# Seven block products in the second input projection: five rwkv blocks and three gate pairs, ten gate tiles left to the weave

## The chip, the cores and the metric

One NeuronCore of one Trainium2 chip runs the kernel. The metric is the device time of one execution in microseconds. TensorE (PE) multiplies, VectorE (DVE), ScalarE (ACT) and GpSimd (POOL) do the rest, and SyncE (SP) issues all DMAs from one queue.

## The reference

Two transformer-like blocks run one behind the other on 1024 tokens of 1024 channels, in float32. The change lies in the second block's input projection, cut here to what matters:

```
h = rmsnorm_2(x, g_mix)
z = h @ w_in                       # 1024 x (672 + 1792 + 2048) columns
z_mla, z_rwkv, z_gate = split(z)
z_rwkv = z_rwkv + (shifted by one token - z_rwkv) * mu_rwkv
gate = sigmoid(z_gate)
y_a = mla_branch(z_mla, ...)       # attention over two scaled latents, q and kv
y_b = rwkv7_branch(z_rwkv, ...)    # r, k, v of 512 columns each, ranks of 256
x = x + (gate_a * y_a + gate_b * y_b) @ w_out
```

## The kernel before

Every large product is made of three float32r matmuls: hi x hi, hi x lo and lo x hi, where ScalarE rounds an operand to its hi part (`split_hi`) and VectorE subtracts to get the lo part (`split_lo`). Activations stand transposed (channels on partitions, tokens along the row) as `op`, hi and lo of eight 128-channel tiles. A matmul multiplies a 128x128 weight tile with 512 tokens (one half) into one of eight PSUM banks, which `tile_of` hands out in turn.

The projection stage has one generator for each engine (`z_sync`, `z_tensor`, `z_scalar`, `z_vector`, `z_gpsimd`), and the engines meet by semaphores only; each works through its own list in order. Its blocks of 256 output columns come in the order: three of the latents (`lat`), then seven of rwkv (`rwkv_blocks` = 6, 2, 3, 0, 1, 4, 5). `dense` (L892 to L894) makes a block of 4 output tiles of 128x512 from 8 channel tiles, 96 matmuls. Between the matmuls of rwkv blocks one and two `norm_q` and `norm_kv` put the column sums and the spread of the latents' norms on PE. VectorE drains each bank to `z_row` with the token scale `rs`, and shifts a tile by two operations (`z_shift`, a subtraction at L183 and a scalar_tensor_tensor at L193). SyncE stores it to DRAM. The latents are scaled in place in `lat` by `scale_latent` and stored for later.

The 2048 gate columns are not made there. `wkv_tensor` blends 32 half tiles of gates (24 matmuls each, L2591 to L2593; `gate_steps`, tiles in `wt_g`) with `weave(front, back)`: four of them ahead (`GATE_LEAD`), the others spread evenly over 16 steps of the first front alone and 20 steps of each of four backs. A front prepares a pair of rwkv heads (ranks, norms, decays, mostly on VectorE and ScalarE, with single matmuls between); the back of pair p makes its scores while the front of pair p+1 runs. So each front has a chain PE, ScalarE, VectorE, PE, and the gate products stand between its links in PE's list. VectorE drains each gate half with `rs`, ScalarE takes the sigmoid (L2608).

A seven-product form exists already (class `Sevens`, `sevenfold`, `seven_products`, used by both feed-forwards, L915 to L918). It splits channels, columns and tokens in two each and makes 7 products of 4 channel tiles, 128 columns and 512 tokens, 84 matmuls, where 8 blocks take 96. It needs four sums of weight quarters (`add_all`), seven hi and lo parts of weights, seven forms of the moving operand (`x`), and sums of the products: of each pair ScalarE keeps three banks (`kept`) and VectorE adds the others. In the feed-forward three weight buffers stand in turn.

## Time and profile before

| what | us |
|---|---|
| three runs, lowest, median, highest | 2754.94, 2759.53, 2760.14 |
| the profiled execution | 2758.2 |
| its span from the first to the last instruction | 2756.4 |
| PE busy | 2645.3 (96%) |
| VectorE, ScalarE, GpSimd busy | 1792.2, 987.7, 400.3 |

A stretch is read by the table of busy time (Rows 2): PE's busy time against the length tells whether PE has gaps. A matmul's record is longer than its turn, since matmuls overlap: the distance of two starts is what one costs. A row of the timeline gives start, duration, engine, line, operation, tiles, shape and count, and in brackets the idle time before it with what ended it.

### The profile page before, as it was taken

The page shows a single profiled execution, that of the slowest core. Times are in us where ns is not written, and L with a number is a line of the kernel's source. Part 1 is how long each engine was busy: PE and PEld are TensorE (multiplying, and loading weights), DVE is VectorE, ACT ScalarE, POOL GpSimd, SP SyncE. Part 2 cuts the span into 40 slices and gives each one's busy share as a digit, 9 for nine tenths or more (in the row PEclk, how much of TensorE's full clock was granted, in tenths as well). Part 3 has the DMA queues.
Part 4 walks back from the last instruction along what each step waited for, and adds up shares of the span by engine and source line. Part 5 has one row for each costly group of instructions (what it writes and reads, how often), then busy time and mean ns, then how long its engine had stood idle before and what let it go on. Part 6 is the DMA issues. An engine that isn't in the chain of part 4 may idle for free.

```text
span 2756.4 us, 37636 instructions
## 1 busy us (share of the span) xinstructions
PE 2645.3 (96%) x15032; PEld 2140.6 (78%) x15032; DVE 1792.2 (65%) x2291; ACT 987.7 (36%) x1352; POOL 400.3 (15%) x345
## 2 busy tenths in 40 slices
PE   7989999999999999999999899889999999999998
PEld 6777888888787878877778577678888887888876
DVE  7795677777666565445553856645498886766554
ACT  5244443333333421024444543332343233433422
POOL 2001122222200000000002602303112221000211
PEclk9999999999999999999999999989999999999999
DMA  5332223233487513245557234243234447986411
GB/s 192 48 115 99 77 85 110 97 111 104 149 317 278 186 62 136 88 138 151 170 156 208 61 81 167 93 161 135 87 125 148 162 149 252 347 325 218 143 40 62
DMA packets 302445, 401.93 MB, mean 146 GB/s; under 512 B 66017, under 2 KB 180577, under 8 KB 299969
## 3 DMA queue, kind: packets, MB, share of 16 engines
q1 hardware_dynamic: 302272, 399.53, 42.8%
q8 instruction: 120, 1.97, 0.3%
q14 instruction: 53, 0.43, 0.0%
HBM read 278.51 MB, written 121.21 MB: 145 GB/s over the span
## 4 chain that ended last, share of the span: by engine, by line
PE 83%; DVE 9%; ACT 3%; issue 3%; DMA 1%; POOL 1%; SPq 0%; DVEq 0%; ACTq 0%; POOLq 0%
PE bank L915 8%; PE bank L918 8%; PE bank L916 8%; PE bank L1986 6%; PE bank L892 6%; PE bank L1987 6%; PE bank L1988 6%; PE bank L893 6%; PE bank L894 6%; PE bank L2591 2%; PE bank L3326 2%; PE bank L2592 2%; PE bank L2593 2%; PE bank L3356 1%; PE bank L4051 1%
## 5 line engine op out<-in xcount | busy, mean ns | idle before, releaser
L915 PE MATMUL bank<-hi,hi 128*128 128x512 f32 x1008 | 393.0, 390 | 2.7 <-ACT kept L2042 1.4
L183 DVE TENSOR_TENSOR w_lo<-w_raw,w_hi 128x2048 fp32r<-128x2048 f32 (+4 forms) x123 | 256.0, 2097 | 142.7 <-ACT w_hi L480 98.2
L1986 PE MATMUL bank<-w_hi,w_hi 128*128 128x512 f32 x756 | 296.3, 392 | 9.1 <-DVE w_lo L183 6.6
L1987 PE MATMUL bank<-w_lo,w_hi 128*128 128x512 f32 x756 | 295.7, 391 | 0.0
L1988 PE MATMUL bank<-w_hi,w_lo 128*128 128x512 f32 x756 | 295.6, 391 | 0.0
L892 PE MATMUL bank<-op_hi,w_hi 128*128 128x512 f32 x608 | 238.9, 393 | 2.4 <-DVE gates L950 1.5
L893 PE MATMUL bank<-op_lo,w_hi 128*128 128x512 f32 x608 | 237.4, 390 | 0.0
L894 PE MATMUL bank<-op_hi,w_lo 128*128 128x512 f32 x608 | 237.4, 390 | 0.0
L918 PE MATMUL bank<-hi,block_lo 128*128 128x512 f32 x576 | 224.1, 389 | 0.0
L916 PE MATMUL bank<-block_lo,hi 128*128 128x512 f32 x576 | 224.1, 389 | 0.0
L915 PEld LDWEIGHTS bank<-hi,hi 128*128 128x128 f32 x1008 | 189.4, 188 | 43.6 <-ACT kept L2042 2.2
L183 POOL TENSOR_TENSOR sq_sum<-sq_sum,sq 128x1024 f32<-128x1024 f32 (+1 forms) x33 | 70.0, 2121 | 1013.6 <-ACT sq L735 1012.2
L183 POOL TENSOR_TENSOR f_out<-f_out,rs 128x512 f32<-128x512 f32 x78 | 129.0, 1653 | 416.8 <-DVE f_out L183 362.4
L183 DVE TENSOR_TENSOR block_lo<-block,hi 128x512 fp32r<-128x512 f32 (+1 forms) x168 | 133.3, 803 | 82.7 <-ACT hi L580 75.4
L2042 ACT ACTIVATE kept<-bank 128x512 f32<-128x512 f32 x108 | 64.6, 598 | 330.1 <-PE bank L918 330.0
L1986 PEld LDWEIGHTS bank<-w_hi,w_hi 128*128 128x128 f32 x756 | 142.8, 189 | 40.6 <-DVE w_lo L183 7.8
L916 PE MATMUL bank<-sum_lo,hi 128*128 128x512 f32 x432 | 168.1, 389 | 0.0
L918 PE MATMUL bank<-hi,sum_lo 128*128 128x512 f32 x432 | 168.1, 389 | 0.0
L1988 PEld LDWEIGHTS bank<-w_hi,w_lo 128*128 128x128 f32 x756 | 142.9, 189 | 29.8
L1987 PEld LDWEIGHTS bank<-w_lo,w_hi 128*128 128x128 f32 x756 | 143.0, 189 | 29.6
L183 DVE TENSOR_TENSOR hT<-hT,bank 128x512 f32<-128x512 f32 x88 | 58.2, 684 | 120.1 <-PE bank L1988 62.7
L892 PEld LDWEIGHTS bank<-op_hi,w_hi 128*128 128x128 f32 x608 | 114.7, 189 | 27.3 <-issue 3.4
(518 smaller groups left out, 5563.3 us busy)
## 6 DMA issues: line engine op xcount, KB each, us to landing
f_scratch<-f_out SPq DMA_DIRECT2D x189, 256.0 KB, 2.0
w_raw<-f_scratch SPq DMA_DIRECT2D x42, 1024.0 KB, 9.7
w_raw<-in_w_ffn_down SPq DMA_DIRECT2D x28, 1024.0 KB, 5.7
record<-record_scratch SPq DMA_DIRECT2D x16, 1024.0 KB, 5.4
block<-in_w_ffn_up SPq DMA_DIRECT2D x16, 1024.0 KB, 5.5
w_raw<-in_w_down SPq DMA_DIRECT2D x14, 1024.0 KB, 5.3
w_raw<-in_w_in SPq DMA_DIRECT2D x13, 1024.0 KB, 6.2
block<-in_w_gate SPq DMA_DIRECT2D x11, 1024.0 KB, 5.2
```

Source lines behind the costliest of these rows:

```text
L183: return e.tensor_tensor(out, x, y, op)
L892: t.matmul(ps[:], hi[:, k, wc], x[0][:, k, xc], start=n == 0, stop=False)
L893: t.matmul(ps[:], hi[:, k, wc], x[1][:, (k + turn) % KD, xc], start=False, stop=False)
L894: last = t.matmul(ps[:], lo[:, k, wc], x[0][:, k, xc], start=False, stop=n == kt - 1)
L915: t.matmul(ps[:], w.hi(q, n)[:, j, :], x.hi(i, n)[:, j, :], start=start, stop=False, skip_group_check=more)
L916: t.matmul(ps[:], w.hi(q, n)[:, j, :], x.part(i, n, lo=1)[:, j, :], start=False, stop=False, skip_group_check=more)
L918: last = t.matmul(ps[:], w.part(q, n, lo=1)[:, j, :], x.hi(i, n)[:, j, :], start=False, stop=end, skip_group_check=more)
L1986: t.matmul(ps[:], ws[0][:, j, wc], xs[0][:, j, :], start=start, stop=False, skip_group_check=more)
L1987: t.matmul(ps[:], ws[0][:, j, wc], xs[1][:, j, :], start=False, stop=False, skip_group_check=more)
L1988: last = t.matmul(ps[:], ws[1][:, j, wc], xs[0][:, j, :], start=False, stop=stop, skip_group_check=more)
L2042: s.activation(F.kept[n // 2][:], psum.tile(F.name, "x", q)[:], ACT.Copy).then_inc(*A.up("kept", q, n))
L2591: t.matmul(ps[:], hi[:, k, :], op[0][:, k, hs(half)], start=k == 0, stop=False)
```

## The change

Of the seven rwkv blocks two (6 and 2) stay plain. Behind them eight pairs of column tiles are made in seven products: three gate pairs (tiles 0 to 5) and then the rwkv blocks 3, 0, 1, 4, 5. The weights come by `Sevens` with two buffers of 1 MB (`w_z`), a pair's load waiting for the last product of two pairs before. The moving operand has seven forms (`xz`): three are blocks of `op`, four (2, 3, 4, 5) are made during the plain blocks, each 128 x 4 x 512: GpSimd makes three sums of blocks and the three operations of form 5, VectorE three subtractions and four lo parts, ScalarE four hi parts. Each is waited for by the first pair's product that uses it.

For each pair ScalarE keeps three banks, VectorE makes four halves of `z_row` (one with `rs`, three sums), GpSimd multiplies the three sums by `rs`. VectorE shifts an rwkv pair (`pair_shift`) behind the pair's last product, ScalarE takes a gate pair's sigmoid there (`gated`). The weights of the first two woven gate tiles are split behind the last shift. The column sums of both latents now lie in plain block one and only the spread for kv in block two. The store of the latents has three semaphores in place of one, and the loads of ranks, masks and the first r and k are split in two groups (`load_ranks`, `load_first`) behind products of the last two pairs. The weave gets ten gate tiles, 20 halves, spread over the same steps.

```diff
@@ class Memory
+        self.w_z = self.sevens(P, 4, tuple(66 + n for n in range(7)), [(s, (s + 4, s + 5, s + 6)) for s in (82, 9)])
+        self.x_z = {n: (at(lo, "x_raw", [P, 4, HALF]), at(hi, "x_hi", [P, 4, HALF], F32R), at(lo, "x_lo", [P, 4, HALF], F32R))
+                    for n, lo, hi in ((2, 90, 94), (3, 98, 78), (4, 18, 22), (5, 26, 30))}
@@ build
-    plan += [wblock(w_in2, 0, KD, MLA_COLS + 256 * i, 256) for i in rwkv_blocks]
+    plan += [wblock(w_in2, 0, KD, MLA_COLS + 256 * i, 256) for i in rwkv_blocks[:PLAIN_BLOCKS]]
...
-                   [wblock(w_in2, 0, KD, MLA_COLS + RWKV_COLS + P * i, P) for i in range(16)], before)
+                   [wblock(w_in2, 0, KD, MLA_COLS + RWKV_COLS + P * i, P) for i in range(2 * GATE_PAIRS, 16)], before)
...
+    z_pairs = [("gate", g) for g in range(GATE_PAIRS)] + [("rwkv", b) for b in rwkv_blocks[PLAIN_BLOCKS:]]
+    z_order, z_last = list(sevenfold(len(z_pairs))), len(z_pairs) - 1
...
+    def turned_over(k):
+        q, n = z_order[k]
+        return [(q1, n1) for q1, n1 in ([(q, 0)] if n == 2 else []) + ([z_order[k - 1]] if k and z_order[k - 1][1] else [])
+                if q1 < z_last]
@@ z_sync
+            if 0 <= pair < z_last - 1:
+                q.wait_ge(*Sz.T.of("zup", pair, 6))
+                wz.load(q, pair + 2, pair_source(pair + 2))
...
+            store_rows(m)
@@ z_tensor
+        for q, n in z_order:
+            if n == 2:
+                t.wait_ge(*A.of("z kept", q, 0))
+            if n == 4:
+                t.wait_ge(*A.of("z kept", q, 2))
+            if n == 5:
+                t.wait_ge(*A.of("z kept", q, 4))
+            if n == 6:
+                t.wait_ge(*V.of("z sum", q, 4))
+            if q == 0 and n in mem.x_z:
+                t.wait_ge(*V.of("form lo", n))
+            seven_products(t, T, "zup", "zs", q, n, wz, xz, 0)
@@ z_scalar
+        form_hi(2)
+        landed(s, *d_lat)
+        form_hi(4)
+        s.wait_ge(*wt1.used(B_RWKV + 1))
+        form_hi(3)
...
+            for q1, n1 in turned_over(k):
+                s.wait_ge(*T.of("zup", q1, n1))
+                wz.split_hi(s, q1 + 1, n1)
+            if k and z_order[k - 1][1] == 6:
+                gated(z_order[k - 1][0])
@@ z_vector
+        rows_out(0)
         v.wait_ge(*V.last())
+        shift(0, 0)
+        shift(0, 1)
+        scale_latent("kv", 3, 2, vec["g_kv_a_2"])
+        yield
+        landed(v, *d_xk)
+        wz.landed(v, 1)
+        wz.add_all(v, 1)
+        for n in (0, 1):
+            wz.split_lo(v, 0, n)
+        landed(v, d_lat[1])
+        for n, x, y, row, col in ((4, x_raw[2], x_raw[3], 1, 1), (3, x_raw[3], mem.x_even[:], 0, 0), (2, x_raw[2], x_raw[3], 1, 1)):
...
+            tt(v, x_raw[n], x, y, ALU.subtract).then_inc(*V.up("form", n))
+        form_lo(2)
+        for n in (2, 3, 4):
+            wz.split_lo(v, 0, n)
+        form_lo(4)
+        rows_out(1)
+        form_lo(3)
+        shift(1, 0)
+        shift(1, 1)
+        yield
+        for k, (q, n) in enumerate(z_order):
+            if n == 2 and 1 < q + 1 <= z_last:
+                wz.landed(v, q + 1)
+                wz.add_all(v, q + 1)
+            for q1, n1 in turned_over(k):
+                wz.split_lo(v, q1 + 1, n1)
+            if k and z_order[k - 1][1] == 6:
+                pair_shift(z_order[k - 1][0])
+            if n in Z_HALVES:
+                z_sum(q, n)
+            if k == 3:
+                form_lo(5)
+                for j in (5, 6):
+                    wz.split_lo(v, 0, j)
+            yield
+        pair_shift(z_last)
+        wt_g.split_lo(v, 0)
+        wt_g.split_lo(v, 1)
@@ z_gpsimd
+        block(x_raw[2], 1, 1)
...
+        block(x_raw[3], 0, 1)
+        g.wait_ge(*Sz.T.of("cols q"))
+        block(mem.x_even[:], 0, 0)
+        landed(g, *d_lat)
+        g.wait_ge(*Sz.A.of("form hi", 2))
+        tt(g, x_raw[5], op_block(0, 1, 0), xz.hi(0, 2), ALU.subtract).then_inc(*G.up())
...
+        tt(g, x_raw[5], x_raw[5], op_block(1, 1, 0), ALU.add).then_inc(*G.up())
...
+        tt(g, x_raw[5], x_raw[5], xz.part(0, 2), ALU.subtract).then_inc(*G.up("form", 5))
+        for q, n in z_order:
+            if n in (1, 4, 6):
+                g.wait_ge(*Sz.V.of("z sum", q, n))
+                tt(g, z_part(q, n), z_part(q, n), rs[:, hs(Z_HALVES[n][1])], ALU.mult).then_inc(*G.up("z rs", q, n))
@@ gates
-    gate_tiles = [(i, half) for i in range(16) for half in range(2)]
+    GATES = 16 - 2 * GATE_PAIRS
+    gate_tiles = [(i, half) for i in range(GATES) for half in range(2)]
```

## Rows read from the trace of the kernel before

**Rows 1.** The page: its header line, and busy time of each engine.

```profile
span 2756.4 us, 37636 instructions
...
PE 2645.3 (96%) x15032; PEld 2140.6 (78%) x15032; DVE 1792.2 (65%) x2291; ACT 987.7 (36%) x1352; POOL 400.3 (15%) x345
```

**Rows 2.** Table by stretch: length, busy PE, PEld, DVE, ACT, POOL; clock, DMA, GB/s.

```profile
1091.30:1200.70 109.40, 109.36 (x483) 90.25 (x482) 51.31 (x50) 11.07 (x7) 0.00 (x0) 1.00 0.38 132
...
1222.60:1264.40 41.80, 37.57 (x161) 28.52 (x162) 25.18 (x28) 20.79 (x24) 0.00 (x0) 0.96 0.43 132
1264.40:1322.80 58.40, 57.89 (x530) 45.09 (x529) 33.98 (x44) 28.59 (x38) 0.00 (x0) 1.00 0.52 156
1322.80:1385.30 62.50, 59.07 (x530) 46.19 (x528) 33.95 (x44) 25.41 (x35) 0.00 (x0) 0.97 0.54 160
```

**Rows 3.** Timeline of PE: start, duration; at half clock and in the projection.

```profile
995.33 0.63 PE L892 MATMUL bank<-op_hi,w_hi 128*128 128x512 f32 x1
995.75 0.63 PE L893 MATMUL bank<-op_lo,w_hi 128*128 128x512 f32 x1
...
1100.03 0.39 PE L892 MATMUL bank<-op_hi,w_hi 128*128 128x512 f32 x1
1100.26 0.39 PE L893 MATMUL bank<-op_lo,w_hi 128*128 128x512 f32 x1
```

**Rows 4.** The table by stretch again, of seven products in the feed-forward.

```profile
540.00:559.04 19.04, 19.04 (x86) 15.77 (x85) 13.21 (x17) 6.70 (x13) 5.00 (x3) 1.00 0.25 84
```

**Rows 5.** Timeline of VectorE and GpSimd, in feed-forward and projection.

```profile
546.49 0.68 DVE L183 TENSOR_TENSOR block_lo<-block,hi 128x512 fp32r<-128x512 f32 x1
547.09 1.78 DVE L183 TENSOR_TENSOR f_out<-f_out,gate 128x512 f32<-128x512 f32 x1
...
546.65 1.67 POOL L183 TENSOR_TENSOR f_out<-f_out,rs 128x512 f32<-128x512 f32 x1 [7.23 <-DVE f_out L183]
...
1067.48 1.29 DVE L183 TENSOR_TENSOR z_row<-bank,rs 128x512 f32<-128x512 f32 x2
1068.80 3.22 DVE L183 TENSOR_TENSOR z_shift<-z_row 128x1024 f32<-128x1024 f32 x1
...
1067.43 1.04 POOL L2551 COPY gates<-cos_sin 32x1024 f32<-32x1024 f32 x1 [21.89 <-DVE z_row L2516]
1068.55 2.39 POOL L183 TENSOR_TENSOR gates<-gates,cos_sin 32x1024 f32<-32x1024 f32 x1
```

**Rows 6.** VectorE groups of one shape in the feed-forward, 340 to 760.

```profile
L183 DVE TENSOR_TENSOR block_lo<-block,hi 128x512 fp32r<-128x512 f32 x81 | 55.4, 684 | 48.8 <-ACT hi L580 48.8
```

**Rows 7.** The same of the projection, 985 to 1205.

```profile
L183 DVE TENSOR_TENSOR w_lo<-w_raw,w_hi 128x2048 fp32r<-128x2048 f32 x9 | 21.6, 2404 | 5.7 <-ACT w_hi L480 5.7
...
L193 DVE SCALAR_TENSOR_TENSOR z_shift<-z_shift,vec_cols,z_row 128x1024 f32<-128x1024 f32 x13 | 16.7, 1284 | 0.5
```

**Rows 8.** Groups of all engines, 1042 to 1091.3: ScalarE and GpSimd.

```profile
L480 ACT ACTIVATE w_hi<-w_raw 128x2048 fp32r<-128x2048 f32 x2 | 3.8, 1906 | 0.0
...
L183 POOL TENSOR_TENSOR sq_sum_kv<-sq_sum_kv,sq 128x1024 f32<-128x1024 f32 x1 | 2.4, 2411 | 21.2 <-ACT sq L735 21.2
```

**Rows 9.** Timeline of VectorE: latent q is scaled.

```profile
1062.37 3.68 DVE L193 SCALAR_TENSOR_TENSOR lat<-lat,vec_cols,lat_rs 128x1024 f32<-128x1024 f32 x3 [0.45 <-ACT lat_rs L955]
```

**Rows 10.** DMA issues of the projection, 985 to 1205: median us to landing.

```profile
w_raw<-in_w_in SPq DMA_DIRECT2D x7, 1024.0 KB, 5.8
```

**Rows 11.** Timeline of VectorE, then PE, at the end of pair 1's front.

```profile
1306.10 0.69 DVE L183 TENSOR_TENSOR k_score<-bank,wkv_mask 128x512 f32<-128x512 f32 x1 [3.13 <-PE bank L2803]
...
1312.35 1.23 DVE L183 TENSOR_TENSOR w_lo<-w_raw,w_hi 128x1024 fp32r<-128x1024 f32 x1 [2.08 <-ACT w_hi L480]
...
1317.61 1.22 DVE L183 TENSOR_TENSOR t<-k,t 128x1024 f32<-128x1024 f32 x1
...
1296.35 1.98 PE L2773 MATMUL bank<-t,headones 128*128 128x512 f32 x4
...
1322.79 1.03 PE L2784 MATMUL bank<-ident,a 128*128 128x128 f32 x8
```

More of the change, by code:

```diff
@@ L587, in split_lo, with __init__, hi, part @@
             *self.V.up(self.name, "lo", i, n, part))
+class Forms:
+    def __init__(self, hi, lo):
+        self.high, self.low = hi, lo
+    def hi(self, i, n):
+        return self.high[n]
+    def part(self, i, n, lo=1):
+        return self.low[n]
 class Sets:
@@ L2397, in z_sync @@
+            if pair == z_last:
+                load_first(q)
+            store_rows(m)
         yield
     def load_ranks(q):
-        q.wait_ge(*wt1.used(B_RWKV + 5))
+        q.wait_ge(*Sz.T.of("zup", z_last - 1, 6))
+        q.wait_ge(*Sz.V.of("z sum", z_last, 1))
         q.wait_ge(*Sz.T.of("cols kv"))
-        landed(q, *d_xk, d_lat)
-        for i in (12, 13):
-            q.wait_ge(*d_zs[i % 2].of(i))
+        landed(q, *d_xk, *d_lat)
+        wt_g.load(q, 1)
+        for c in range(2):
+            q.wait_ge(*d_zs[c].of(*z_label("rwkv", 6, c)))
@@ L2508, in z_vector, with shift @@
                 yield
-        wt1.lo_at(v, B_RWKV)
+        def shift(m, c):
+            kind, b = row_blocks[m]
+            i = 2 * b + c
+            row, t, mu = mem.z_row[c], mem.z_shift[c], vec["mu_rwkv_2"][:, i:i + 1]
+            if m < PLAIN_BLOCKS:
+                v.wait_ge(*V.of("rwkv", i, 1))
+            shift_free(v, m, c)
+            tt(v, t[:], row[:, 0:L], row[:, 1:L + 1], ALU.subtract).then_inc(*V.up())
+            v.wait_ge(*V.last())
+            stt(v, t[:], t[:], mu, row[:, 1:L + 1], ALU.mult, ALU.add).then_inc(*V.up("shift", *z_label(kind, b, c)))
@@ new lines, in row_read, with rows_out @@
+        def row_read(m, c):
+            if m:
+                kind, b = row_blocks[m - 1]
+                v.wait_ge(*(V if kind == "rwkv" else A).of("shift", *z_label(kind, b, c)))
+        def rows_out(m):
+            kind, b = row_blocks[m]
+            for c in range(2):
+                row_read(m, c)
+                for half in range(2):
+                    v.wait_ge(*T.of("rwkv", 2 * b + c, half))
+                    tt(v, mem.z_row[c][:, 1 + half * HALF:1 + half * HALF + HALF], psum.tile("rwkv", 2 * b + c, half)[:],
+                       rs[:, hs(half)], ALU.mult).then_inc(*V.up("rwkv", 2 * b + c, half))
+                    psum.drained(V, "rwkv", 2 * b + c, half)
@@ new lines, in pair_shift @@
+        def pair_shift(q):
+            if z_pairs[q][0] == "rwkv":
+                v.wait_ge(*Sz.G.of("z rs", q, 4))
+                v.wait_ge(*V.of("z sum", q, 5))
+                shift(q + PLAIN_BLOCKS, 1)
+                v.wait_ge(*Sz.G.of("z rs", q, 6))
+                shift(q + PLAIN_BLOCKS, 0)
+        wt1.lo_at(v, B_RWKV)
+        landed(v, d_cs)
+        v.wait_ge(*V.of("lat", 5, 1))
+        tt(v, cos_sin[64:128, :], kpe[64:128, :], cos_sin[64:128, :], ALU.mult).then_inc(*V.up("kpe"))
```

208 lines of the change are left out of this document (138 added, 70 removed).

## The prediction

> **What bounds the kernel now.** I read the page's header and busy shares first: TensorE is busy 96% of a span of 2756.4 us, VectorE 65% [rows 1]. Then the table of busy time by stretch, cut where the stages of this change begin and end [rows 2]. From 1091.3 to 1200.7 five blocks of the input projection run and PE has no gap. From 1200.7 on the 32 half tiles of gates are woven into the rwkv fronts and backs. There PE still works almost without a break: 37.57 us of 41.80, 57.89 of 58.40, 59.07 of 62.50. So both stages are bound by PE; the gates are what fills PE while VectorE and ScalarE work through a front. The PE timeline gives the price of a 128x512 matmul as the distance of two starts, 0.227 us, and not the 0.39 us of the record; at half clock it is 0.43 [rows 3]. The seven-product form already runs in the feed-forward: 84 matmuls in 19.04 us without a gap, beside 13.21 us of VectorE and 5.00 us of GpSimd [rows 4].
>
> **Matmuls saved.** A block of 256 columns costs 96 matmuls, a pair in seven products 7 x 4 x 3 = 84. Eight pairs save 96 matmuls, 96 x 0.227 = 21.8 us. In their places: the projection had 480 matmuls (108.8 us) behind its second plain block and gets 672 (152.3), +43.5; the weave loses 12 of its 32 gate products of 24, 288 matmuls, -65.3.
>
> The rest of the sum is what PE has to wait for. It turns on one thing, told first.
>
> **Two engines, one port.** In the feed-forward a GpSimd multiply starts at 546.65 and takes 1.67 us; the VectorE operation already running ends at 547.17, and the next one, begun at 547.09, takes 1.78 us where its like takes 0.68 [rows 5, 6]. It ends 0.55 us behind GpSimd. At 1068.80 the same: 3.22 us where 1.22 is usual, 1.1 us past the end of a GpSimd operation. So a GpSimd operation waits for the VectorE operation in flight, then VectorE stands until it is through. Operations with an operand in a bank aren't held up: z_row, from a bank, took 1.29 for two at 1067.48 beside a GpSimd copy. The Trainium skill, "SBUF — State Buffer", section "Who interferes with whom", says this of VectorE instructions with two SBUF inputs against a GpSimd one that reads SBUF: the second to issue fully blocks. The rows agree; by that rule the time would be 2796, without it that of the second rival, 2767.
>
> **Start of the seven products.** The operand forms are tiles of 4 x 512 = 2048 elements. VectorE takes 2.28 us for one (the nine of 2.40 on average include held-up ones) [rows 7], 0.68 for 512 elements [rows 6]; ScalarE 1.9; GpSimd takes 2.41 for 1024, so I estimate 4.7 for 2048 [rows 8]. GpSimd's three block sums (from 1054 on, each 4.7) hold up the scaling of latent q, which ended at 1066.05 [rows 9] and now ends at about 1072. Then VectorE drains block one (2.5), shifts two tiles (5.1), scales latent kv (3.2): 1083. From there it has in order: four sums of pair 1 (2.9), two lows (1.4), forms 4, 3, 2 (6.8): 1094.1. ScalarE turns form 2 over (1.9): 1096.1. GpSimd waits for the store of latent kv, which has landed by 1089 (1 MB takes 5.8 [rows 10]), and starts its first operation for form 5 there. VectorE still owes the low of form 2 (2.3), three weight lows (2.1), the low of form 4 (2.3), four drains (2.5), the low of form 3 (2.3): 11.5 us, with three GpSimd operations of 4.7 between them, 14.1 us. So form 3 is ready at about 1121.7. PE ends plain block two at 1092, does products 0 and 1 to 1097.4, gets product 2's second operand at 1108.6 (11.2 us of waiting) and product 3's at 1121.7 (10.4). Two more waits follow, since two shifts (5.1) and form 5's low stand ahead of the next weights: 0.9 and 2.8. Sum 25.3 us. If nothing is held up, the same list ends at 1106.3 and the waits are 8.7. I take 25.3, as the rows of the lock are exact.
>
> **The rwkv pairs.** A pair gives PE 19.04 us. VectorE has seven lows, four sums and four drains, 15 x 0.69 = 10.3, and for an rwkv pair two shifts of 1.22 + 1.28 [rows 7, 11], 5.0 more; GpSimd's three multiplies hold it for up to 1.2 each, 3.5. That is 18.8 of 19.04, and the order decides: between the end of product (q-1, 6) and the first product of pair q+1 PE has 4 x 2.72 = 10.9 us. VectorE must in that time drain (0.7), split (0.7), stand for GpSimd (1.2), shift twice (5.0), drain (0.7), form four sums with GpSimd between (2.9 + 1.2), wait for ScalarE's copy (0.7), split (0.7): 13.9. PE stands 3.1 us, in the three iterations where weights are formed and an rwkv pair is shifted (q = 4, 5, 6): 9.2. Without the lock 0.7 each, 2.2. In iterations behind a gate pair the 1 MB load, issued at the end of (q-1, 6), is landed after 5.8 us [rows 10]; sums, copy and split end at about 10.5: hidden, with 0.4 us to spare. ScalarE has 7 copies, 3 kept banks and for gate pairs two sigmoids, under 9 us of 19: never the bound. One further wait of 0.9 for a kept bank in the last pair. Here 10.1 us in all.
>
> **The handover to the weave.** Before, the two weight lows of the gates were made ahead of the last shifts and PE went from 1200.7 on without a gap [rows 2]. Now VectorE's queue ends in: drain (0.7), GpSimd's turn (1.2), two shifts (5.0), and only then the low of gate tile 0 (1.2). PE stands 8.3 us (7.1 without the lock).
>
> **The weave.** A pair was 62.5 us with 6.25 gate products; now it has 3.75, so 48.9 if PE stays the bound. The front of pair 1 ended on VectorE at 1318.83, and its rows had their turn on PE at 1322.79: 4.0 us to spare [rows 11]. Between PE's product at 1296.35 and these rows stood three gate products; for pair 1 one is left. That takes 10.9 us from under a chain that was 20 us long, of which 5.2 us were waits (3.1 at 1306.10, 2.1 at 1312.35 [rows 11]) and about 3 gate work: some 2.5 us become visible. Following the queues of all four engines for each pair with the rows' durations, I get waits of 2.1, 2.5 and 1.5 us ahead of the rows, 4.0 ahead of the norm's transposes (cover: one product, now gone) and 2.5 ahead of the r-k sum, 20 us in the whole weave where the same reckoning gives 8.6 for the kernel before. Exposed: +11. Bounds: 0 if the chain shrinks with its waits; if it doesn't shrink at all, a pair is up to 6 us over 48.9, 24 for four.
>
> **Clock.** Where PE had just stood waiting for the norms of the latents' blocks, matmuls were 0.43 us apart at 995.33, not 0.227 [rows 3]: half clock, PE's low level of 1.2 GHz. Three waits of 8 us and more (two at the start, one at the handover) can bring that back. Eight matmuls at half clock lose 1.6 us, and I take one or two groups of that size for each wait: 5 for all, from 0 to 8.
>
> **Moved for nothing.** The latent stores, the rank and mask loads and the first r, k loads sit elsewhere in SyncE's queue. The late ones are issued with (7, 3) and land some 6 us later, ahead of four lead gate products of 21.8 us; were they late by more than 20 us, the rank matmuls would wait. SyncE's new waits for (q, 6) have only the pair's load and two stores behind them, whose row tiles are wanted a pair later.
>
> **Sum.** -21.8 + 25.3 + 10.1 + 8.3 + 11 + 5 = +37.9. Against the profiled execution (2758.2, span 2756.4) that is 2796; the median of the runs is 1.3 above that execution, so it changes nothing. I say 2796.
>
> **Rivals.** (1) The forecast, 2784 to 2808. Chance 0.62. (2) GpSimd and VectorE hardly hold each other up, as the long forms yield or VectorE is ahead of them: -21.8 + 8.7 + 3.1 + 7.1 + 11 + 1 = +9, 2767, between 2761 and 2780. For it: no row shows an operation of 2048 elements on GpSimd. Against: a 1024 one held VectorE to its end. Chance 0.15. (3) The weave loses its cover altogether, +24 in place of +11: 2809, from 2804 to 2815. For it: PE idles 4.2 us already in the first front, where only two products lie over the norm [rows 2]. Chance 0.13. (4) Faster: PE stays the bound in the projection, since VectorE gets through the forms before PE is through the plain blocks. It decides at the low of form 3: if that stands within 3 us of 1100, start waits are about 3, and with short weave waits -21.8 + 3 + 2 + 7 + 3 = -7, 2751. Against: VectorE's list up to that low is 38 us from 1083 on. Chance 0.08. That the matmuls aren't saved I exclude by counting them in the loop. The rest, 0.02, is some queue I misread.
>
> **Chances.** A measurement of this kernel tells about 0.2% (5.5 us) from nothing. Faster by more 0.06, within 0.05 (the edges of rivals 2 and 4), slower 0.89. Range 2765 to 2811: it takes rival 2 from its middle and the near part of rival 3, and leaves out about 0.2.
>
> **What would show it.** In the trace after: 672 matmuls on the seven-product lines between the plain blocks and the first gate; PE waits of about 10 us for VectorE's lows ahead of products 2 and 3 of pair 0; VectorE form operations of 5 to 7 us in place of 2.3 beside GpSimd ones of about 5; three waits of about 3 us for the weights of pairs 5, 6, 7; a wait of about 8 us at the first gate; a weave of some 232 us for 286 to 289. The forecast is wrong if the forms are ready at 1100, or if the weave is shorter than 225 or longer than 245 us.

## The result, and the profile after

| | kernel before | kernel after |
|---|---|---|
| median of four executions each | 2757.74 us | 2815.61 us |
| lowest and highest | 2754.94, 2760.14 | 2809.09, 2817.17 |
| profiled execution, its span | 2758.2, 2756.4 | 2809.1, 2807.1 |

The ratio is 1.0204, with a 95% interval of 1.0191 to 1.0217: 2% slower, 57.9 us where 37.9 were forecast. The forecast was 2796 us and its range ended at 2811; the direction was right, the size not. Four more executions of the same kernel later gave 2810.6 to 2814.1. Over all eight the median is 2813.1, and the experiments are held against that.

Header and busy times of the page after:

```profile
span 2807.1 us, 37824 instructions
...
PE 2644.9 (94%) x14936; PEld 2137.4 (76%) x14936; DVE 1875.0 (67%) x2375; ACT 1020.1 (36%) x1417; POOL 468.2 (17%) x375
```

PE has 96 matmuls less, as meant, and yet its busy time is the same 2645 us as in [rows 1]: a record is longer at half clock (0.63 us for 0.39). Half clock means a granted clock of 0.5 in the table. The table by stretch (length; busy time of PE, PEld, VectorE, ScalarE, GpSimd; granted clock, DMA share, GB/s) of the eight pairs up to the first gate product, the four gates ahead of the first front, the first front, and everything from the projection's first matmul to the q projection:

```profile
1096.02:1293.15 197.13, 163.90 (x674) 132.31 (x672) 138.37 (x144) 57.49 (x86) 52.58 (x27) 0.91 0.28 99
1293.15:1317.80 24.65, 24.65 (x97) 19.87 (x97) 6.32 (x7) 5.84 (x7) 0.00 (x0) 0.88 0.24 82
1317.80:1359.60 41.80, 35.88 (x155) 24.73 (x155) 22.77 (x25) 24.42 (x32) 0.00 (x0) 0.96 0.44 131
...
960.15:1545.04 584.89, 513.78 (x3266) 413.42 (x3264) 361.63 (x401) 196.17 (x266) 78.31 (x35) 0.93 0.37 120
```

The last stretch in the kernel before:

```profile
962.73:1492.35 529.62, 511.42 (x3362) 413.42 (x3360) 278.62 (x317) 163.26 (x201) 10.62 (x5) 0.98 0.42 133
```

This stretch holds all of the difference: 584.9 us for 529.6. The rest of the kernel is 4.6 us shorter in this trace, 2222.2 us for 2226.8. That is a difference of executions: in the traces of the experiments, which leave this part alone, it is 2220.8 to 2226.3. In the first stretch of [rows 2] PE had no gap and a clock of 1.00; here, over the eight pairs, it is busy 163.9 us of 197.1, at 0.91. PE's timeline at four of its waits, with two more matmuls behind the last (in brackets the idle time):

```profile
1106.14 0.76 PE L936 MATMUL bank<-x_hi,hi 128*128 128x512 f32 x1 [4.52 <-DVE sum_lo L183]
...
1122.71 0.80 PE L936 MATMUL bank<-x_hi,hi 128*128 128x512 f32 x1 [11.28 <-DVE x_lo L183]
...
1210.54 0.77 PE L936 MATMUL bank<-op_hi,hi 128*128 128x512 f32 x1 [2.77 <-DVE block_lo L183]
...
1293.15 0.80 PE L2823 MATMUL bank<-op_hi,w_hi 128*128 128x512 f32 x1 [8.11 <-DVE w_lo L183]
1293.74 0.63 PE L2824 MATMUL bank<-op_lo,w_hi 128*128 128x512 f32 x1
1294.17 0.63 PE L2825 MATMUL bank<-op_hi,w_lo 128*128 128x512 f32 x1
```

These are product 2 and product 3 of pair 0, the first product of pair 5, and the first gate. Behind each, matmuls are 0.43 us apart and not 0.227: half clock [rows 3]. Pairs 6 and 7 repeat the third row, at 1234.01 and 1257.70. VectorE, then GpSimd, ahead of the first two:

```profile
1098.77 2.29 DVE L183 TENSOR_TENSOR x_lo<-x_raw,x_hi 128x2048 fp32r<-128x2048 f32 x1 [1.98 <-ACT x_hi L2539]
1100.98 5.01 DVE L183 TENSOR_TENSOR sum_lo<-sum,hi 128x512 fp32r<-128x512 f32 x1
1105.92 5.04 DVE L183 TENSOR_TENSOR block_lo<-block,hi 128x512 fp32r<-128x512 f32 x1
1110.88 4.99 DVE L183 TENSOR_TENSOR sum_lo<-sum,hi 128x512 fp32r<-128x512 f32 x1
1115.79 2.28 DVE L183 TENSOR_TENSOR x_lo<-x_raw,x_hi 128x2048 fp32r<-128x2048 f32 x1
...
1098.90 6.54 POOL L183 TENSOR_TENSOR x_raw<-op_hi,x_hi 128x2048 f32<-128x2048 f32 x1 [33.75 <-ACT x_hi L2539]
1105.52 4.88 POOL L183 TENSOR_TENSOR x_raw<-x_raw,op_lo 128x2048 f32<-128x2048 f32 x1
1110.48 4.83 POOL L183 TENSOR_TENSOR x_raw<-x_raw,x_lo 128x2048 f32<-128x2048 f32 x1
```

Three operations of 0.68 us [rows 6] last 5.0 each, and each ends some 0.5 us behind the GpSimd operation beside it. The same lock struck once where the prediction didn't look, at 1051 (VectorE, then GpSimd, then PE):

```profile
1051.34 4.90 DVE L183 TENSOR_TENSOR sum<-block,sum 128x512 f32<-128x512 f32 x1
1056.16 0.15 DVE L966 COPY norm_cols<-bank 128x8 f32<-128x8 f32 x1
...
1050.84 9.78 POOL L183 TENSOR_TENSOR x_raw<-op_hi,op_lo 128x2048 f32<-128x2048 f32 x2
...
1056.37 0.27 PE L961 MATMUL bank<-ones,sq_sum_kv 128*128 128x1 f32 x1 [3.66 <-DVE norm_cols L966]
```

The copy of latent q's column sums stood behind the held-up sum, and PE, which wanted their place for those of kv, stood until 1056.37, 4.05 us from its last start. In the weave PE waits ahead of the rows (where [rows 11] had nothing at 1322.79), the norm's transposes, the kv products, the kk2 sums and the r-k sum:

```profile
1326.30 0.87 PE L2999 MATMUL bank<-ident,t 128*128 128x128 f32 x3 [2.53 <-DVE t L3174]
...
1349.91 0.30 PE L3016 MATMUL bank<-ident,a 128*128 128x128 f32 x1 [1.51 <-DVE a L183]
...
1370.14 0.45 PE L2999 MATMUL bank<-ident,t 128*128 128x128 f32 x1 [1.65 <-DVE t L3174]
...
1398.34 0.37 PE L3053 MATMUL bank<-duo,duo 64*64 64x64 f32 x2 [2.88 <-ACT rest L3139]
...
1417.37 0.47 PE L2991 MATMUL bank<-headones,t 128*128 128x2 f32 x3 [2.38 <-DVE t L183]
...
1436.56 0.67 PE L3005 MATMUL bank<-t,headones 128*128 128x512 f32 x1 [2.25 <-DVE t L193]
```

Not all of these are new. The kernel before has waits of the same kinds and sizes in its weave (total us, times, longest; norm, kv products, r-k sum), and 15.3 us in all by the distances of starts, where this one has 31.2:

```profile
PE bank L2767 <- DVE t L2942: 3.7, 3, 2.5
PE bank L2821 <- ACT rest L2907: 3.3, 2, 2.9
PE bank L2773 <- DVE t L193: 2.2, 1, 2.2
```

The first line above, the norm of pair 0, is one that stood before. New in kind are the waits ahead of the rows and of the kk2 sums.

### The profile page after: what moved, and what is told of

Read it like the earlier page. It is cut to its first block, busy times and chain, and to the rows that moved or that the text cites. A ratio compares the mean times of both kernels' runs of the same rounds, so it can differ in the third digit from the quotient of the medians.

```text
span 2807.1 us, 37824 instructions
## 1 busy us (share of the span) xinstructions
PE 2644.9 (94%) x14936; PEld 2137.4 (76%) x14936; DVE 1875.0 (67%) x2375; ACT 1020.1 (36%) x1417; POOL 468.2 (17%) x375
## 4 chain that ended last, share of the span: by engine, by line
PE 76%; DVE 14%; issue 4%; ACT 3%; DMA 2%; POOL 1%; SPq 1%; DVEq 0%; ACTq 0%; POOLq 0%
PE bank L936 9%; PE bank L937 9%; PE bank L939 9%; PE bank L2007 6%; PE bank L2009 6%; PE bank L2008 6%; PE bank L913 4%; PE bank L914 4%; PE bank L915 4%; PE bank L3558 2%; DVE w_lo L183 1%; PE bank L3588 1%; PE bank L4283 1%; PE bank L4285 1%; PE bank L4284 1%
## 5 line engine op out<-in xcount | busy, mean ns | idle before, releaser
L183 DVE TENSOR_TENSOR w_lo<-w_raw,w_hi 128x2048 fp32r<-128x2048 f32 (+3 forms) x112 | 237.3, 2136 | 108.3 <-ACT w_hi L485 62.3
L183 DVE TENSOR_TENSOR block_lo<-block,hi 128x512 fp32r<-128x512 f32 (+1 forms) x200 | 160.3, 813 | 89.9 <-ACT hi L585 82.1
L913 PE MATMUL bank<-op_hi,w_hi 128*128 128x512 f32 x448 | 177.0, 395 | 2.4 <-DVE gates L971 1.5
L914 PE MATMUL bank<-op_lo,w_hi 128*128 128x512 f32 x448 | 175.6, 392 | 0.0
L915 PE MATMUL bank<-op_hi,w_lo 128*128 128x512 f32 x448 | 175.4, 391 | 0.0
L585 ACT ACTIVATE hi<-block 128x512 fp32r<-128x512 f32 x176 | 108.8, 625 | 101.2 <-PE bank L939 48.6
```

What stands on the lines that cost most here:

```text
L183: return e.tensor_tensor(out, x, y, op)
L585: s.activation(self.hi(i, n, js), self.part(i, n, js), ACT.Copy).then_inc(*self.A.up(self.name, "hi", i, n, part))
L913: t.matmul(ps[:], hi[:, k, wc], x[0][:, k, xc], start=n == 0, stop=False)
L914: t.matmul(ps[:], hi[:, k, wc], x[1][:, (k + turn) % KD, xc], start=False, stop=False)
L915: last = t.matmul(ps[:], lo[:, k, wc], x[0][:, k, xc], start=False, stop=n == kt - 1)
```

## How the experiments are read

For each kernel PE's timeline from the projection's first matmul to the q projection is split in three. *Waits* are all distances of two matmul starts above 0.6 us, less the 0.227 that one costs. *Half* is the time at which the granted clock was half. *Other* is what the stretch's length has changed by against the kernel before, less the change of the waits, less 0.227 us for each matmul more (or plus for each less). It is the half clock: split by whether the granted clock was half when a matmul started, the distances under 0.6 us, less those of the same two kinds of matmul at full clock, add up to 25.5 us more than before inside half clock and 3.0 less outside it in the first trace (other 22.7), and to 7.9 more and 0.6 less in e15 (other 7.4). A wait that falls in half clock costs nothing more by it, so the time at half clock is more than twice what it costs.

| kernel | median us | ratio to before (95%) | stretch | waits | half | other |
|---|---|---|---|---|---|---|
| before | 2757.7 | | 529.6 | 20.7 | 20.5 | 0 |
| after, first trace | 2815.6 | 1.0204 (1.0191, 1.0217) | 584.9 | 75.1 | 85.3 | 22.7 |
| e13 after again | 2811.5 | 1.0197 (1.0183, 1.0211) | 587.0 | 75.6 | 88.7 | 24.3 |
| e1 filled waits, projection | 2807.9 | 1.0184 (1.0169, 1.0199) | 584.3 | 50.1 | 51.2 | 14.0 |
| e14 filled waits, weave | 2808.5 | 1.0187 (1.0173, 1.0200) | 582.0 | 62.5 | 61.4 | 15.1 |
| e15 both filled | 2801.0 | 1.0158 (1.0144, 1.0173) | 577.0 | 32.1 | 34.1 | 7.4 |
| e2 handover, both tiles | 2811.1 | 1.0195 (1.0180, 1.0211) | 585.5 | 80.5 | 88.7 | 17.9 |
| e5 handover, tile 0 | 2802.7 | 1.0156 (1.0141, 1.0171) | 578.0 | 69.7 | 78.5 | 21.2 |
| e3 shifts | 2796.5 | 1.0139 (1.0120, 1.0158) | 571.3 | 65.7 | 75.1 | 18.6 |
| e4 form 5 | 2807.7 | 1.0186 (1.0168, 1.0203) | 584.8 | 75.2 | 78.5 | 22.4 |
| e6 no gate pair | 2799.8 | 1.0149 (1.0132, 1.0166) | 570.5 | 61.3 | 64.9 | 14.0 |
| e7 lead of one | 2809.5 | 1.0181 (1.0166, 1.0196) | 582.6 | 73.8 | 88.7 | 21.7 |
| e8 three together | 2785.8 | 1.0097 (1.0081, 1.0112) | 560.9 | 56.5 | 61.4 | 17.2 |
| e9 and new start | 2775.1 | 1.0057 (1.0044, 1.0070) | 546.8 | 48.3 | 47.8 | 11.4 |
| e10 no gate pair | 2765.0 | 1.0022 (1.0013, 1.0031) | 540.6 | 35.7 | 41.0 | 9.6 |
| e11 two pairs, lead of one | 2768.2 | 1.0032 (1.0019, 1.0044) | 540.5 | 41.5 | 47.8 | 9.1 |
| e12 one pair, lead of one | 2772.0 | 1.0044 (1.0032, 1.0056) | 546.6 | 40.9 | 47.8 | 13.2 |

## The experiments

### The clock: filled waits (e1, e14, e15) and a second trace (e13)

After the first trace the theory was that the waits had been forecast about right and the clock behind them not; the rival was a cost elsewhere. The added matmuls (fillers) stand ahead of a wait and last about as long:

```diff
+        FILL = {(0, 2): 20, (0, 3): 48, (5, 0): 14, (6, 0): 14, (7, 0): 14}
+        def filler(ps, count):
+            for j in range(count):
+                t.matmul(ps[:], xz.hi(0, 0)[:, j % 4, 0:P], xz.hi(0, 0)[:, j % 4, :], start=True, stop=True)
```

> The kernel after, and in addition 146 matmuls that nothing reads: PE issues them ahead of the waits (20 ahead of product 2 and 48 ahead of product 3 of pair 0, 14 ahead of each of the pairs 5, 6, 7, 36 ahead of the first gate product), into a bank that the next product starts anew. They last about as long as each wait (4.5, 10.9, 3 x 3.2, 8.2 us at 0.227 us each), so the path through VectorE is untouched and PE no longer stands still. Theory A (the clock that falls after each wait is the term that was sized too small: 36.5 us at half clock between 1104 and 1299, 10.2 us lost there by the count of 512-column matmuls): half-clock time there falls below 10 us and the time by 7 to 10 us, to about 2807. Rival B (the clock costs no more than the 5 us forecast, the missing 20 us are elsewhere): 0 to -3 us, 2813 to 2816. If the added matmuls themselves get in the way of the path, the time rises.

The table by stretch of this kernel, the pairs, the four gates and the weave:

```profile
1096.50:1292.02 195.52, 188.85 (x819) 154.03 (x818) 138.13 (x144) 57.44 (x85) 52.84 (x27) 0.99 0.29 101
1292.02:1314.03 22.01, 22.01 (x97) 17.94 (x97) 6.32 (x7) 5.92 (x7) 0.00 (x0) 1.00 0.24 82
1314.03:1544.92 230.89, 199.41 (x1922) 156.42 (x1921) 127.44 (x165) 102.19 (x139) 0.00 (x0) 0.93 0.53 158
```

The clock stays at 0.99 and 1.00 where it was 0.91 and 0.88. The four gates take 22.0 us for 24.65. But the pairs take only 1.6 us less: behind product 3 PE, now at full speed, stands 0.86 us for pair 1's first product and 2.51 for product 5 of pair 0, where it had stood 0.7. Half clock costs nothing where VectorE's next low is late anyway. So of 10 us some 4 came back, and the weave was 3.7 us longer in this trace. The time fell by 5.2 us (2807.9 for 2813.1), which lies between the two theories.

> The kernel after with 76 matmuls that nothing reads, issued ahead of eight waits of the weave (ahead of the norm's transposes of pairs 0 and 1, the rows of pairs 0 and 2, the sums kk2 and rk of pairs 2 and 3; 4 to 12 each, about as long as the waits, 18 of the weave's 36 us of gaps), into the bank that the waiting product has already opened. Theory A (of the 22.7 us that the weave is longer than its matmuls, half clock is about 5): half clock in the weave falls from 27.3 to below 10 us and the time by 3 to 5 us, 2811. Rival B (the chains bound the weave, so a faster clock only makes the waits longer): no more than -1, and the unfilled waits grow by what the matmuls save.

```diff
             ps = tile_of(t, "low", "kk2", p)
+            filler(ps, "kk2", p)
             t.wait_ge(*V.of("kk2", p))
```

The same stands ahead of the other seven waits. The table by stretch of the weave, and then of the whole stretch with both sets (e15):

```profile
1318.36:1543.76 225.40, 209.53 (x1998) 163.61 (x1997) 127.15 (x165) 102.34 (x139) 0.00 (x0) 0.98 0.54 162
```

```profile
959.30:1536.32 577.02, 548.02 (x3488) 442.25 (x3486) 360.77 (x401) 196.19 (x266) 78.54 (x35) 0.97 0.38 122
```

> Both sets of matmuls that nothing reads, 146 in the projection and 76 in the weave. Theory A (the clock's share of the 20 us by which the forecast fell short is about 10): 2815 less 8 less 4, about 2804. Rival B (what the projection gains the first front takes back, as the first such run showed: projection -4.3, weave +3.7): 2808 or more.

Half clock in the weave fell from 27.3 to 10.2 us and the time by 4.6, as theory A had it. With both sets the clock of the stretch is 0.97 and the time 2801.0, 12.1 us less than after, though PE issues 222 matmuls that nothing uses. By the spread of the executions that is good to some 4 us either way; in the traces the stretch is 7.9 us shorter than in the first of the kernel after and 10.0 shorter than in its second. So the clock is worth some 12 us by experiment, against the 5 forecast. The column "other" fell by 15.3, from 22.7 to 7.4; the 50.4 us of fillers took the place of only 43.0 us of waits, which makes up the difference to the 7.9 of the traces. Half clock didn't go altogether: 34.1 us are left for 20.5 in the kernel before, and with them the 7.4.

> The kernel after itself once more, for a second trace. Its four times were 2809.1 (the profiled one) and 2815.2 to 2817.2. Theory A (the same waits give one, two or three groups of half clock behind them, by chance from run to run): a median of 2813 to 2816 again, and a second trace in which the waits before the q projection are the same to 0.1 us in the projection, while the half-clock time and the lengths of projection and weave differ by several us. Rival B (the first trace is typical and the times differed by the chip): median 2809 to 2811.

The second trace of the same kernel has the same waits (11.74, 4.90, 3 x 3.16, 8.50 us) and a projection of 357.7 us for 357.6. Its weave was 229.3 for 227.2 us, with 30.7 us at half clock for 27.3:

```profile
1317.53:1546.81 229.28, 199.58 (x1922) 156.31 (x1921) 127.45 (x165) 102.35 (x139) 0.00 (x0) 0.93 0.52 159
```

So nearly the same waits bring more or less half clock; one of the weave's, ahead of the norm of pair 0, was also 3.7 us for 2.8. The weave accounts for 2 us of the spread between executions; the rest of it stays open. The median, 2811.5, lies between the two theories.

### The waits, one by one (e2 to e5)

e2 makes the lows of gate tiles 0 and 1 ahead of the last drain and the shifts:

```diff
+            if (q, n) == (z_last, 6):
+                wt_g.split_lo(v, 0)
+                wt_g.split_lo(v, 1)
...
-        wt_g.split_lo(v, 0)
-        wt_g.split_lo(v, 1)
```

> VectorE makes the lows of the first two woven gate tiles ahead of its last drain and the last pair's shifts, ScalarE their highs behind the last kept bank. Theory A: the wait of 8.5 us at the first gate product goes, with it the half clock behind it (5.8 us, 2.4 us lost): -10.9, about 2805. Rival B: the same work is only moved: the last two rows of rwkv and with them the first front's loads come 2.4 us later, and what PE gains at the first gate it gives back in the first front (-5 or less, 2811).

The wait at the gate went and came back at the ranks (VectorE, then PE):

```profile
1281.53 1.22 DVE L183 TENSOR_TENSOR w_lo<-w_raw,w_hi 128x1024 fp32r<-128x1024 f32 x1
1292.63 1.23 DVE L183 TENSOR_TENSOR w_lo<-w_raw,w_hi 128x1024 fp32r<-128x1024 f32 x1 [9.88 <-ACT w_hi L485]
...
1312.14 1.19 PE L2979 MATMUL bank<-lo_rank,w2a 64*128 64x512 f32 x1 [6.37 <-ACT g_rank L3071]
```

Tile 1's weights landed only at 1291.5, and the last shifts stood behind them. The seven distances behind it are 1.0 us at half clock, so they too count as waits in the table. The time fell by 2 us, which the measurement can't tell from nothing. e5 moves tile 0 alone.

> As the handover kernel, but only the first woven gate tile's high and low are made ahead of the last drain and shifts; the second's stay behind them. In the handover kernel the second tile's weights had landed only at 1291.5, VectorE stood 9.9 us for them with the last shifts queued behind, and PE's wait reappeared at the rank products (6.75 us and seven of about 1 us). Theory A: that queue order ate the gain, and now the wait of 8.5 us at the first gate and the half clock behind it go for good: -8 to -11, 2805 to 2808. Rival B: the first front is bound by something later than the gates (the loads of ranks, r and k, issued up to 1283): PE waits there instead, -4 or less.

It gave -10.5 us (2802.7), theory A: the wait is gone, and PE waits 0.9 us for the ranks.

e3 splits the shift of an rwkv pair in two:

```diff
                 shift(q + PLAIN_BLOCKS, 1)
+                yield
                 v.wait_ge(*Sz.G.of("z rs", q, 6))
                 shift(q + PLAIN_BLOCKS, 0)
...
+                shifting = pair_shift(z_order[k - 1][0])
+                next(shifting, None)
+            if n == 2:
+                if q:
+                    for _ in shifting:
+                        pass
+                z_sum(q, 1)
```

> Behind an rwkv pair VectorE shifts the second tile before, and the first tile behind, the four weight sums and two lows of the next pair but one (the sum for product 1 moves behind the shift too). The first shift then lies in the 5.8 us in which the weights land. Theory A: the three waits of 3.16 us ahead of pairs 5, 6 and 7 go, -9.5, and with them some 10 us at half clock, -3 to -4: about 2803. Rival B: VectorE is full (18.8 of 19.04 us for each pair by the prediction), so the wait only turns up a product or two later, at the next weights or a kept bank: -3 or less, 2812 and up.

All three waits are gone. VectorE now stands for the weights, ahead of the sums, and then makes the lows at once; the pairs as a whole:

```profile
1184.94 0.69 DVE L183 TENSOR_TENSOR sum<-block 128x512 f32<-128x512 f32 x1 [4.40 <-DMA block<-in_w_in]
...
1188.64 1.29 DVE L183 TENSOR_TENSOR block_lo<-block,hi 128x512 fp32r<-128x512 f32 x2 [0.83 <-ACT hi L585]
...
1097.26:1281.35 184.09, 159.41 (x674) 128.92 (x672) 142.59 (x144) 57.79 (x85) 54.86 (x27) 0.93 0.30 105
```

The pairs are 13.0 us shorter: 9.5 of the three waits, 0.7 of one ahead of product 5, and the rest clock (25.4 us of half clock for 35.2). The median fell by 16.6 us. Rival B is refuted.

e4 gives form 5 to VectorE:

```diff
+        wz.split_lo(v, 1, 0)
+        tt(v, x_raw[5], op_block(0, 1, 0), xz.hi(0, 2), ALU.subtract).then_inc(*V.up())
...
+        form_lo(5)
...
-        tt(g, x_raw[5], op_block(0, 1, 0), xz.hi(0, 2), ALU.subtract).then_inc(*G.up())
```

> The three operations of form 5 are taken from GpSimd and made by VectorE (2.28 us each) behind the low of form 3, then the low of form 5 and the weights of products 5 and 6, and only then the two shifts. Nothing of GpSimd then stands beside VectorE's sums and lows. Theory A (the port: VectorE operations of 5.01, 5.03 and 4.98 us fall to 0.68): the waits of 4.91 and 11.74 us ahead of products 2 and 3 shrink together by 13 us to about 3.7, and a new one of about 4 us comes ahead of product 5: -9 us of waits and 2 of clock, about 2804. Rival B (VectorE's operations are long there for another reason, such as their operands' place): they stay at 5 us, and the three added operations make it slower, 2820 or more.

```profile
1100.48 0.68 DVE L183 TENSOR_TENSOR sum_lo<-sum,hi 128x512 fp32r<-128x512 f32 x1
1101.08 0.68 DVE L183 TENSOR_TENSOR block_lo<-block,hi 128x512 fp32r<-128x512 f32 x1
1101.68 0.68 DVE L183 TENSOR_TENSOR sum_lo<-sum,hi 128x512 fp32r<-128x512 f32 x1
```

The same three operations in the same place, 0.68 us each with GpSimd idle: the lock is shown. By the Trainium skill, "SBUF — State Buffer", section "Who interferes with whom", the second to issue fully blocks; the trace agrees, 5.01 for 0.68. The waits ahead of products 2 and 3 fell from 16.6 to 5.9 us. Two others grew, 2.7 ahead of product 5 and 6.9 ahead of product 6, where VectorE made form 5 and both shifts first. The time fell by 5.4 us (some 5 either way), half of what I had expected.

### The gates' worth (e6, e7)

```diff
-(6, 2, 3, 0, 1, 4, 5), 2, 3
+(6, 2, 3, 0, 1, 4, 5), 2, 0
```

> No gate pair in the seven products: five rwkv pairs only, all 16 gate tiles woven as in the kernel before (the two weight buffers change places, since the last pair is now an even one). 60 matmuls are saved instead of 96, which by itself is 8.2 us slower than the change. Theory A (the gates are worth more in the weave than their matmuls: the trace after shows the weave 22.7 us longer than its matmuls explain, where 11 was forecast): the weave is back at 268 to 270 us from the first rank product to the q projection, the start waits and three waits of 3.2 us stay, and the time falls by 22.7 - 8.2 = 14.5 us, to about 2801. Rival B (the exposure is the 11 us of the forecast): -3, 2813. Rival C (the weave's waits come from something other than the missing gate products, such as the later loads): it stays long, +8, 2824.

```profile
1259.11:1531.71 272.60, 256.53 (x2209) 202.56 (x2209) 142.62 (x183) 118.87 (x159) 0.00 (x0) 0.97 0.53 157
```

With its gates back the weave is 272.6 us (before 269.8) and its waits 17.7 for 31.2; the time fell by 13.3 us although PE has 36 matmuls more, 8.2 us. So taking six gate tiles out of the weave costs about 22 us on top of the matmuls that it saves there. The same comparison with the new start (e9 and e10 below) gives 10.1 + 8.2, 18 us. The start and the three waits for weights stood as before, now ahead of pairs 2, 3 and 4.

e7 has the three gate pairs, and one gate ahead of the first front:

```diff
-    GATE_LEAD, GATE_STEPS = 4, len(gate_tiles) + 2
+    GATE_LEAD, GATE_STEPS = 1, len(gate_tiles) + 2
```

> One gate product ahead of the first front instead of four; the three others are spread over the weave, 19 there in place of 16. The work is the same. Theory A (each product missing from the weave shows 1.5 us of its chain, 18 us for 12): -4.5 in the weave, but the ranks are then wanted 16 us earlier, at about 1299, when ScalarE has them by 1305 at the earliest, so PE waits some 6 us there: together about +1, 2811 to 2819, with the waits behind the first front clearly fewer. Rival B (the waits in the weave don't depend on how many gate products lie over them): the waits behind the first front stay at the same sum and the rank wait comes on top, +6 or more.

```profile
1301.44 0.69 PE L2977 MATMUL bank<-lo_rank,w2a 64*128 64x512 f32 x1
```

The time fell by 3.6 us. The ranks were there in time (no idle at 1301.44), so my reckoning of ScalarE's queue was wrong. But the three gates brought the weave's waits only from 31.2 to 30.4 us, not the 4.5 less of 1.5 us for each product. The cover isn't a sum per product: it depends on the link over which a product comes to stand.

### Together (e8 to e12)

> Three things together on the kernel after: the split shifts (alone -19), only tile 0's low ahead of the last shifts, and form 5 made by VectorE, with the sum for product 1 between the two shifts. Theory A (the three are waits at different places of one path, so they add): -19 -10 -6, about 2781. Rival B (what comes earlier only waits at the next place, above all in the weave, as with the added matmuls, where the projection got 4.3 us shorter and the weave 3.7 longer): 2790 or more.

The three (split shifts, tile 0's lows early, form 5 on VectorE) give -27.3 us together, 2785.8, where their own runs add up to -32.5: between the theories. The weave took back 2 us of it, as it had with the fillers; the other 3 are open. e9 orders the start anew:

```diff
-        wz.add_all(v, 0)
         latent_column("q", 0)
         latent_column("kv", 1)
+        wz.add_all(v, 0)
...
-        form_lo(2)
-        for n in (2, 3, 4):
-            wz.split_lo(v, 0, n)
-        form_lo(4)
-        rows_out(1)
-        form_lo(3)
+        for n in (2, 3):
+            wz.split_lo(v, 0, n)
+        form_lo(2)
+        form_lo(4)
+        form_lo(3)
+        wz.split_lo(v, 0, 4)
+        rows_out(1)
```

> The kernel with three things together, and the start set in a new order: pair 0's weight sums behind the latents' columns; weight lows 2 and 3 in the 2 us in which VectorE stood for ScalarE's first high form; the low of form 3 ahead of plain block two's drains; the sum for product 4 ahead of the first tile's shift. Before this edit PE stood 4.05 us for the kv columns, then 1.65, 4.21, 1.57 and 6.88 us ahead of products 2, 3, 5 and 6 of pair 0, 18.4 in all. Theory A (all of it is the order of VectorE's queue, with no more work than PE covers): about 5 us are left, -13 and 1 or 2 of clock: 2785.8 -> 2771. Rival B (VectorE has more to do between 1083 and 1135 than PE gives it time for, whatever the order): the waits move to the next products and 10 us or more are left, 2778 or more.

```profile
1099.40 0.68 PE L936 MATMUL bank<-x_hi,hi 128*128 128x512 f32 x1 [2.73 <-ACT kept L2584]
...
1117.83 0.77 PE L936 MATMUL bank<-x_hi,hi 128*128 128x512 f32 x1 [5.63 <-DVE block_lo L183]
```

-10.7 us, between A and B. The wait of 4.05 us for the kv columns is gone (one of 1.0 came at 1068). Left are 3.1 us for ScalarE, which makes three high forms ahead of the first kept bank, and 6.0 for product 5: VectorE's list for the forms is longer than PE's cover, in any order tried.

The last three keep all of this and change the number of gate pairs (0, 2, 1, by the same line as in e6) and, in e11 and e12, the lead to one.

> The kernel with the new start, with no gate pair in the seven products (five rwkv pairs, 16 gate tiles woven). Against the kernel before: 60 matmuls -13.6, start waits about 5, one of 1.1, handover and clock about 3, weave +2 (measured 272.6 for 269.8 with the gates left in it): -3, 2756. Against the kernel with three gate pairs and the same start this would be 15 us less. Theory A (gates taken from the weave cost more than they save): 2752 to 2760. Rival B (the difference between three and no gate pairs, 15.8 us in the runs, was in the start and the projection): 2765 or more.

> New start, two gate pairs (12 gate tiles, 24 halves woven) and one gate product ahead of the first front in place of four, so 23 over the weave where the kernel before has 28. 84 matmuls saved, -19.1; start, handover, clock as with no gate pair, +9; the weave misses 5 products at 1.5 us each, +7.5. Theory A: -3, 2756. Rival B (the weave's waits come with any missing gate): 2765.

> New start, one gate pair (28 halves woven), one gate product ahead of the first front: 27 over the weave, one less than in the kernel before, so the gates come out of the lead and not out of the weave. 72 matmuls saved, -16.3; start, handover and clock +9; weave +1.5 to +3. Theory A (only gates over the weave are worth their place): -5, 2754, the fastest of all. Rival B (the ranks are late when only one gate product stands ahead of them): PE waits there, 2760.

All three came out above their expectations. The nearest, with no gate pair, is 0.22% slower than the kernel before (0.13 to 0.31): in the stretch it saves 13.6 us of matmuls and pays 15.0 in waits and 9.6 in "other". In e11 and e12 the ranks were late after all, as e12's rival B had it, with 6.1 and 6.7 us of idle time at the first rank product: without the wait at the first gate they are wanted sooner, and ScalarE's operations on them stood behind gate tile 1's weights, which had not landed (e11, ScalarE, then PE):

```profile
1248.12 1.06 ACT L485 ACTIVATE w_hi<-w_raw 128x1024 fp32r<-128x1024 f32 x1 [12.29 <-DMA w_raw<-in_w_in]
1249.09 1.04 ACT L3083 ACTIVATE lo_rank<-lo_rank 64x1024 f32<-64x1024 f32 x1
...
1251.22 1.19 PE L2992 MATMUL bank<-lo_rank,w2a 64*128 64x512 f32 x1 [6.09 <-ACT g_rank L3084]
```

No version that was tried beats the kernel before.

## Why the prediction was right and wrong

The sum of the prediction beside the first trace, in us (waits by their change against the kernel before):

| term | forecast | trace |
|---|---|---|
| matmuls saved | -21.8 | -21.8 |
| waits of the projection: start, rwkv pairs, handover | 25.3 + 10.1 + 8.3 = 43.7 | 38.5 |
| waits of the weave | 11 | 15.9 |
| clock (here "other") | 5 | 22.7 |
| rest of the kernel | 0 | -4.6 |
| sum | 37.9 | 50.7 |

The medians are 57.9 us apart (55.4 with all eight executions of the kernel after): the first trace is of the fastest of its four. The second, at 2812.1, has 54.9 us of waits and 24.3 of "other" for a sum of 53.8. What the executions of 2815 to 2817 had more, no trace shows.

**Matmuls saved.** As forecast: 96 less in the page, and a matmul at full clock still costs 0.227.

**Two engines, one port.** Right, shown by e4. I had estimated 4.7 us for a GpSimd operation of 2048 elements; beside the held-up ones they took 4.8 to 4.9, and the first, which had to wait for VectorE's x_lo, 6.5.

**Start.** 21.4 us (4.05 + 4.91 + 11.74 + 0.70) for 25.3, each counted by the distance of two starts. Product 3 began 1.0 us later than I had reckoned. Product 2 waited 4.9 and not 11.2: its low was there at 1106.0 and not 1108.6, since one GpSimd operation stood in its way and not two, and PE came to it 4 us later. These 4 us are the wait at 1056 that the prediction doesn't have: I had let GpSimd's sums hold up the scaling of latent q, but not asked what else stood behind them in VectorE's list.

**The rwkv pairs and the handover.** Three waits of 3.16 for 3.1, one of 1.07 for 0.9, one of 8.50 for 8.3: following VectorE's list between two products with the rows' durations was exact to 0.2 us here. e3 and e5 show that each is a matter of order alone.

**The weave.** 15.9 us for 11; the bounds were 0 to 24. The reckoning was too low on both sides: it gave 8.6 us of waits for the kernel before, whose trace has 15.3, and 20 for this one, which has 31.2. To hold it against the trace of before would have shown that. The links named came out near the reckoning (rows 1.9 and 1.1 for 2.1, 2.5 and 1.5; norm 2.1 for 4.0; r-k sum twice 2.5 for once). What it missed are two waits of 2.4 and 2.7 us ahead of the kk2 sums and 9.1 us ahead of kv products (1398.34, 1448.76, 1507.42, 1541.15), where before those were 3.8; three of the four end with ScalarE's drain of a bank, the one at 1448.76 (1.2 us) with VectorE's `chunk_decay`. With its clock, the missing cover (the gate products that PE had to do while a chain ran) costs about 22 us by e6, 18 by e9 and e10.

**Clock.** This step failed. I charged half clock to the three waits of 8 us and more alone, 5 us for all with bounds of 0 to 8, and put it at nothing for every shorter wait. Counted as above, matmul by matmul, the waits ahead of products 2 and 3 and at the handover lost 2.3, 2.7 and 2.8 us: 7.8, inside my bounds. (Ahead of product 2 the wait was 4.9 us, not 11.) The rest came where I had charged nothing: 3.2 us at the wait of 4.05, 4.7 at the three of 3.16, and 14.5 in the weave for 4.6 before. Six of the eight waits of 2 to 3.1 us in the weave have 3.4 to 6.8 us of half clock about them; the two of 2.5 us ahead of the r-k sums have none. In all, half clock rose from 20.5 us in 4 places to 85.3 us in 14, and the term is 22.7 us for 5; some 12 of it is shown by experiment (e15), the rest by this count.

The warning stood in [rows 2]: the granted clock was 0.96 and 0.97 in two stretches of the weave before, where the longest waits of PE were the 2.5 and 2.9 us of idle time shown above, and each of these two lost 1.5 us. The prediction names half clock at one place only, behind the waits of [rows 3].

That the waits came out at 54.4 us for 54.7 is in part luck: the projection was 5.2 us under the forecast and the weave 4.9 over it.

**Rivals.** Rival 3, the weave without cover, priced it at +24 with a time of 2809; with 15.9 us of waits and 6.8 of clock in the weave the price was right only with the clock in it. Rival 2 fell with e4, rival 4 with the first trace: the low of form 3 was there at 1122.7, not 1100.

**What would show it.** 672 matmuls between 1096 and 1285; the two start waits at their places; the three of 3 us; the one at the gate; forms at 1122. One sign of being wrong came: from the first gate product to the last kv product, where the forecast had some 232 us for 286 to 289 and gave 245 as its limit, the weave took 250.2 us (before 289.7). It became 39.5 us shorter and not 54. From the first rank product on it was 225.5 for 267.8; four lead gates at half clock are the other 2.8 us. VectorE's operations beside GpSimd took 5.0 us.

## What to carry to other kernels

A sum over waits has to carry the clock as a term of its own: in a kernel that PE fills, most new waits of 2 us or more also slowed the matmuls about them, and the clock's share came to two fifths of the waits. The trace of before had it to be read: look at the granted clock about its short waits as well as its long ones. Work that is moved out of a stage in which it covers another engine's chain is worth less than its own time there: of 65 us of gate products taken from this weave, 43 came back. Before an engine gets long side work, write down which queue stands beside it on the same port, item by item, and put the item that PE wants next ahead of it.

## What the hardware showed that I hadn't expected

- Waits of 3.2 us, and most of 2 to 3.1 us, had half clock about them. With filler matmuls in them 41 us of half clock between 1096 and 1318 fell to 3.4, and the granted clock rose from 0.91 to 0.99.
- The same kernel with nearly the same waits had 85.3 us of half clock in the stretch in one execution and 88.7 in another.
- Products of float32 operands (the ranks, 512 columns) stood 0.53 us apart at full clock (e7) and 1.0 behind a wait of 6 us (e2): the clock weighs on them as much.
- A VectorE operation of 512 elements lasted 5.0 us and not 0.68 beside a GpSimd one of 2048, and the copy from a bank in the same queue, which took its 0.15 us at 1056.16 with GpSimd's next operation under way, stood behind it all the same.
